# A decoder layer on one core: x loaded first, the first FFN tile computed k by k, the memory projection between the first two tiles

## The reference

```
x <- x + 1/2 * SwiGLU_1(RMSNorm(x))
h  = RMSNorm(x);  projections of h: stick-breaking q,k,v | dilated q,k,v | memory q | 3 gates
A: stick-breaking attention, B: dilated softmax attention
C: cross-attention into the 256 memory tokens: mn = RMSNorm(mem); mk, mv = split(mn @ w_mem_kv); mk = RMSNorm(mk)
x <- x + (sum over the branches of gate * (branch @ w_br)) @ w_out
x <- x + 1/2 * SwiGLU_2(RMSNorm(x))
```

## Time and profile before

| | |
|---|---|
| time, median of 3 runs | 2578.98 us (2578.18 to 2582.18) |
| profiled execution: its time, its span | 2578.72 us, 2576.8 us |
| busy over the span: PE, DVE, ACT, POOL | 97%, 45%, 22%, 8% |
| mean granted TensorE clock | 0.965 of full speed |
| by the page's chain that ended last: PE, DVE, ACT, DMA | 90%, 5%, 2%, 1% |
| data moved by DMA | 125.80 MB, 49 GB/s on average |

### The profile page before, as it was taken

How to read it: one execution, slowest core, us unless ns; L and a number is a source line. 1 busy time by engine, 2 the same in 40 slices (tenths; PEclk the granted TensorE clock), 3 DMA queues, 4 the chain that set the end, 5 groups by cost and what they waited for, 6 DMA issues and landing times.

```text
span 2576.8 us, 25964 instructions
## 1 busy us (share of the span) xinstructions
PE 2492.7 (97%) x10608; PEld 1944.8 (75%) x10608; DVE 1163.4 (45%) x1185; ACT 577.2 (22%) x716; POOL 194.6 (8%) x153
## 2 busy tenths in 40 slices
PE   6999999999999999889999799999999999999998
PEld 5888888888876555446656688887788888888887
DVE  7344444444455665556611432334534444444444
ACT  5211111111123444433322211122311111111111
POOL 2000000000002454320000000001100000000000
PEclk8999999999999999889956899999999999999999
DMA  5211111111112000000100211113111111111112
GB/s 158 72 49 49 49 49 49 49 49 45 45 48 106 17 17 17 8 25 33 33 1 1 66 51 56 49 49 115 41 50 49 49 49 49 49 49 49 49 49 66
DMA packets 48802, 125.80 MB, mean 49 GB/s; under 512 B 4253, under 2 KB 22461, under 8 KB 48480
## 3 DMA queue, kind: packets, MB, share of 16 engines
q1 hardware_dynamic: 45660, 112.88, 14.0%
q10 hardware_dynamic: 2596, 10.89, 1.2%
q0 software_dynamic: 480, 1.10, 0.3%
HBM read 116.42 MB, written 9.87 MB: 49 GB/s over the span
## 4 chain that ended last, share of the span: by engine, by line
PE 90%; DVE 5%; ACT 2%; DMA 1%; issue 1%; POOL 0%; SPq 0%; DVEq 0%; ACTq 0%; POOLq 0%
PE ps L1121 89%; DVE h_lo L743 1%; PE ps L1423 1%; DMA d_st_keep<-d_st 1%; DVE w_lo L736 1%; DVE xT L908 0%; ACT pr_x L534 0%; ACT pr_x L536 0%; DVE pr_x L850 0%; DMA d_fB<-d_f_keep 0%; DVE xT L791 0%; PE ps L1369 0%; DVE d_qk L858 0%; DVE d_qk L853 0%; DVE h_lo L1063 0%
## 5 line engine op out<-in xcount | busy, mean ns | idle before, releaser
L1121 PE MATMUL ps<-h_hi,w_hi 128*128 128x512 f32 x2240 | 888.6, 397 | 25.9 <-DVE o_dil L1056 14.1
L1121 PE MATMUL ps<-h_lo,w_hi 128*128 128x512 f32 x2240 | 876.4, 391 | 0.0
L1121 PE MATMUL ps<-h_hi,w_lo 128*128 128x512 f32 x2240 | 693.6, 391 | 0.0
L1121 PEld LDWEIGHTS ps<-h_hi,w_hi 128*128 128x128 f32 x2240 | 423.5, 189 | 138.3 <-issue 46.0
L1121 PEld LDWEIGHTS ps<-h_hi,w_lo 128*128 128x128 f32 x2240 | 422.8, 189 | 89.2
L1121 PEld LDWEIGHTS ps<-h_lo,w_hi 128*128 128x128 f32 x2240 | 423.5, 189 | 87.1 <-issue 2.2
L474 ACT ACTIVATE w_hi<-raw 128x1024 fp32r<-128x1024 f32 x196 | 204.1, 1051 | 796.6 <-PE ps L1121 786.7
L736 DVE TENSOR_TENSOR w_lo<-raw,w_hi 128x1024 fp32r<-128x1024 f32 x196 | 252.7, 1297 | 167.2 <-ACT w_hi L474 156.8
L791 DVE TENSOR_TENSOR xT<-xT,ps 128x1024 f32<-128x1024 f32 x176 | 214.5, 1218 | 181.2 <-PE ps L1121 181.2
L1121 PE MATMUL ps<-a_hi,w_hi 128*128 128x512 f32 x704 | 275.7, 392 | 5.6 <-DVE w_lo L736 4.9
L1121 PE MATMUL ps<-a_lo,w_hi 128*128 128x512 f32 x704 | 274.7, 390 | 0.0
(11 more groups left out here) (184 smaller groups left out, 1863.3 us busy)
## 6 DMA issues: line engine op xcount, KB each, us to landing
raw<-in_weights SPq DMA_DIRECT2D x196, 512.0 KB, 3.5
x_nat<-in_x SPq DMA_DIRECT2D x8, 512.0 KB, 7.4
x_keep<-xT ACTq DMA_DIRECT2D x1, 4096.0 KB, 12.4
x_back<-x_keep ACTq DMA_DIRECT2D x1, 4096.0 KB, 12.8
out<-y_nat SPq DMA_DIRECT2D x8, 512.0 KB, 3.2
toe_keep<-toe_row ACTq DMA_DIRECT2D x2, 704.0 KB, 6.5
m_nat<-in_mem SPq DMA_DIRECT2D x1, 1024.0 KB, 5.0
d_fB<-d_f_keep POOLq DMA_DIRECT2D x2, 512.0 KB, 7.5
```

What stands on the lines that cost most here:

```text
L1121: return pe.matmul(o, a, b, start=start, stop=stop, skip_group_check=True)
```

## The change

The change rewrites the start of the program, up to the first round of the FFN loop; what comes after is the same instructions in the same order.

- SP loads only rel, oh, the identity and the gains, and then x, with the first two weight units behind x pieces 0 and 1. The memory, the rest of the constants and the head gains come behind x.
- The units are in another order: gate and up of tile 0 are units 0 and 1, the memory's units are 2, 3, 5 and 7, and gate and up of tile 1 are units 4 and 6.
- PE turns x piece 0, makes toe, turns piece 1, and then goes through k = 0 to 7: it turns piece k + 1 and does the 6 matmuls of tile 0's gate and the 6 of its up product for this k, into pairs 0 and 1. At k = 7 it turns the memory tokens in place of a piece of x. The norm's sum follows behind tile 0.
- The memory products 0 and 1 stand ahead of tile 1's gate product, product 2 between gate and up, product 3 behind up; each `proj_aux` follows at some distance.
- ACT and DVE follow the same order. Temporary buffers move in memory.

Core of the diff:

```diff
@@
-U_MEM = 0
-U_FFN1 = U_MEM + 4
+U_MEM = (2, 3, 5, 7)
+U_FIRST = ((0, 1), (4, 6))
+U_LOOP1 = 8
@@ sync
             sp.dma_start(oh[:], onehot).then_inc(onehot_in, 16)
-            sp.dma_start(m_nat[:], mem.rearrange("(b p) d -> p b d", p=P)).then_inc(mem_in, 16)
-            sp.dma_start(cst[:], consts).then_inc(cst_in, 16)
-            sp.dma_start(hg_raw[:], head_gains).then_inc(hgain_in, 16)
+            sp.dma_start(ident, consts[:, 0, :]).then_inc(ident_in, 16)
             sp.dma_start(g_raw[:], gains).then_inc(gain_in, 16)
-            for r in range(NRAW):
-                sp.dma_start(raw[:, r, :], weights[r]).then_inc(raw_in[r], 16)
             for k in range(DT):
                 sp.dma_start(x_nat[:, k], x[:, k * P:(k + 1) * P].rearrange("(b p) c -> p b c", p=P)).then_inc(x_in[k], 16)
+                if k < NRAW:
+                    sp.dma_start(raw[:, k, :], weights[k]).then_inc(raw_in[k], 16)
+            sp.dma_start(m_nat[:], mem.rearrange("(b p) d -> p b d", p=P)).then_inc(mem_in, 16)
+            sp.dma_start(cst[:, 1:7, :], consts[:, 1:7, :]).then_inc(cst_in, 16)
+            sp.dma_start(hg_raw[:], head_gains).then_inc(hgain_in, 16)
@@ scalar
             split_hi(0)
-            split_hi(1)
+            act.wait_ge(gains_ready, 1)
+            for k in range(DT):
+                act.wait_ge(xT_done, k + 1)
+                gain_hi(k, 0)
+                square(0, k)
+                if k == 0:
+                    split_hi(1)
...
+            split_hi(3)
             rstd(0)
...
-            ffn(0, U_FFN1)
+            proj_square(0)
+            split_hi(4)
+            proj_rstd(0)
+            proj_square(1)
+            split_hi(5)
+            proj_rstd(1)
+            silu_tile(0)
+            split_hi(6)
+            split_hi(7)
+            split_hi(8)
+            silu_tile(1)
+            split_hi(9)
+            ffn(0, U_LOOP1 - 2 * GT)
@@ vector
+            def take_x(k):
+
+                dve.wait_ge(x_turned, k + 1)
+                nc.vector.tensor_copy(xT[:, k, :], ps[:, 1 if k == 0 else 2 + k % 2, :]).then_inc(xT_done, 1)
+
+            take_x(0)
+            dve.wait_ge(toe_done, 1)
...
+            split_lo(0)
+            for k in range(DT):
+                if k + 1 < DT:
+                    take_x(k + 1)
+                gain_lo(0, k, 0)
+                if k == 0:
+                    split_lo(1)
...
+            split_lo(3)
...
+            proj_copy(0)
             newton_rstd(0)
 
             dve.wait_ge(toe_out, 16)
-            ffn(0, U_FFN1, lambda m: gain_lo(1, m - 1, 1) if m else None)
+            proj_copy(1)
+            gate_scale(U_FIRST[0][0], 0)
+            split_lo(4)
+            proj_final(0)
+            up_scale(U_FIRST[0][1], 0)
+            split_lo(5)
+            proj_final(1)
+            glu_product(0, 0)
+            split_lo(6)
+            gate_scale(U_FIRST[1][0], 1)
+            split_lo(7)
+            proj_copy(2)
+            proj_final(2)
+            split_lo(8)
+            up_scale(U_FIRST[1][1], 1)
+            split_lo(9)
+            proj_copy(3)
+            proj_final(3)
+            glu_product(1, 1)
+            ffn(0, U_LOOP1 - 2 * GT, lambda m: gain_lo(1, m - 1, 1) if m else None)
@@ tensor
+            pe.wait_ge(ident_in, 16)
+            turn_x(0)
...
             for k in range(DT):
...
+                if k + 1 < DT:
+                    turn_x(k + 1)
+                else:
+                    pe.wait_ge(m_scaled, MB)
+                    pe.wait_ge(xT_done, DT)
+                    for c in range(DT):
+                        for b in range(MB):
+                            last = pe.transpose(ps[:, 2 + c // 4, (c % 4) * MEM + b * P:(c % 4) * MEM + (b + 1) * P],
+                                                m_nat[:, b, c * P:(c + 1) * P], ident)
...
+                pe.wait_ge(h_ready, k + 1)
+                for part in range(2):
...
+                    last = product(part, part, hh, hl, S, k0=k, k1=k + 1)
...
+            pe.wait_ge(cst_in, 16)
+            norm_sum(0)
+            memory(0)
+            memory(1)
+            pe.wait_ge(newton, 1)
+            proj_aux(0)
+            gate_or_up(0, U_FIRST[1][0], 1)
+            proj_aux(1)
+            memory(2)
+            proj_aux(2)
+            gate_or_up(1, U_FIRST[1][1], 1)
+            memory(3)
+            proj_aux(3)
+            pe.wait_ge(pr_final, PR_SB)
+            ffn(0, U_LOOP1 - 2 * GT, 0)
```

More of the change, by code:

```diff
@@ L200, in layer @@
         rB = at("rB", AR + 68 * K, [P, S])
-        pr_mem = [at(f"pr_mem{i}", AR + (46 + i) * K, [P, MEM]) for i in range(3)]
+        pr_mem = [at(f"pr_mem{i}", AR + (4 + i) * K, [P, MEM]) for i in range(3)]
         pr_x = [at(f"pr_x{i}", AR + (56 + 4 * i) * K, [P, S]) for i in range(3)]
@@ L267, in layer @@
         x_in = [sem(f"x_in{i}") for i in range(8)]
[L268 removed]
+        mem_in, ident_in, cst_in, gain_in, hgain_in = (sem(n) for n in ("mem_in", "ident_in", "cst_in", "gain_in", "hgain_in"))
         onehot_in, rel_in = sem("onehot_in"), sem("rel_in")
@@ L772, in glu_tile, with glu_product @@
                                                op0=ALU.mult, op1=ALU.mult).then_inc(up_scaled, 1)
+            def glu_tile(k, t, slot, i=None, between=None):
+                split_lo(k - 1 + AHEAD, i)
+                gate_scale(k - 1, t, i)
+                split_lo(k + AHEAD, i)
+                up_scale(k, t, i)
+                glu_product(t, slot, i, between)
+            def glu_product(t, slot, i=None, between=None):
+                count = at_turn(t, i, 2 * GT)
                 dve.wait_ge(silu_done, count + 1)
@@ L807, in ffn @@
                 t0, g0, u1 = FT * f, NGRP * f, u0 + 2 * GT
-                for q in range(GT):
-                    glu_tile(u0 + 2 * q + 1, t0 + q, q)
+                if f:
+                    for q in range(GT):
+                        glu_tile(u0 + 2 * q + 1, t0 + q, q)
                 with dve.Fori(0, (NGRP - 1) // 2) as i:
@@ L1141, in hl, with gate_or_up @@
                 return h_lo[:, k, :]
+            def gate_or_up(part, k, t, i=None, there=None):
+                pe.wait_ge(split_done, at_turn(k, i) + 1)
+                after(pe, (gate_scaled, up_scaled)[part], at_turn(t, i, 2 * GT))
+                product(part, k % NW, hh, hl, S, there=there).then_inc(unit_done, 1)
             def gate_up(k, t, i=None, there=None, between=None):
-                for part in range(2):
-                    pe.wait_ge(split_done, at_turn(k, i) + part + 1)
-                    after(pe, (gate_scaled, up_scaled)[part], at_turn(t, i, 2 * GT))
-                    product(part, (k + part) % NW, hh, hl, S, there=there if part == 0 else None).then_inc(unit_done, 1)
-                    if part == 0 and between:
-                        between()
+                gate_or_up(0, k, t, i, there)
+                if between:
+                    between()
+                gate_or_up(1, k + 1, t, i)
             def down(g, k, slot, i=None, finish=None):
@@ L1179, in ffn @@
                 t0, g0, u1 = FT * f, NGRP * f, u0 + 2 * GT
-                gate_up(u0, t0, there=lambda k: pe.wait_ge(h_ready, 8 * r + k + 1), between=lambda: norm_sum(r))
-                for q in range(1, GT):
-                    gate_up(u0 + 2 * q, t0 + q)
+                if f:
+                    gate_up(u0, t0, there=lambda k: pe.wait_ge(h_ready, 8 * r + k + 1), between=lambda: norm_sum(r))
+                    for q in range(1, GT):
+                        gate_up(u0 + 2 * q, t0 + q)
                 with pe.Fori(0, (NGRP - 1) // 2) as i:
@@ L1249, in projections, with turn_x @@
                 proj_aux(n1 - 1)
+            def turn_x(k):
+                pe.wait_ge(x_in[k], 16)
+                if k == 1:
+                    pe.wait_ge(toe_kept, 1)
+                elif k == 2:
+                    pe.wait_ge(toe_kept, 2)
+                elif k:
+                    pe.wait_ge(xT_done, k - 1)
+                for b in range(8):
+                    last = pe.transpose(ps[:, 1 if k == 0 else 2 + k % 2, b * P:(b + 1) * P], x_nat[:, k, b, :], ident)
+                last.then_inc(x_turned, 1)
+            pe.wait_ge(ident_in, 16)
+            turn_x(0)
             pe.wait_ge(onehot_in, 16)
@@ L1269, in _, with memory @@
+                pe.wait_ge(h_ready, k + 1)
+                for part in range(2):
+                    if k == 0:
+                        pe.wait_ge(split_done, part + 1)
+                        if part:
+                            pe.wait_ge(xT_done, 1)
+                    last = product(part, part, hh, hl, S, k0=k, k1=k + 1)
+                    if k == DT - 1:
+                        last.then_inc(unit_done, 1)
+            def memory(n):
                 proj(n, lambda k: mT_hi[:, k, :], lambda k: mT_lo[:, k, :],
@@ L1548, in weight_units @@
 def weight_units(w_mem_kv, f1_gu, f1_down, w_in, w_br, w_out, f2_gu, f2_down):
-    units = column_units(w_mem_kv, range(4)) + swiglu_units(f1_gu, f1_down)
```

(3 more changed lines are left out.)

138 lines of the change are left out of this document (54 added, 84 removed).

## The result

The changed kernel took 2598.25 us (median of 4 runs, 2596.91 to 2599.61) against 2579.03 for the kernel before on the same chip (4 runs): ratio 1.0072, 95% interval 1.0055 to 1.009, so 0.7% slower. The prediction was 2600.4 us, range 2590 to 2609. The profiled execution took 2597.82 us.

What follows compares the result with a forecast made beforehand. The prediction took PE's start of the FFN loop as the bound: 66.0 + 6.4 + 48.6 + 4.5 = 125.5 us, 21.7 later than before. Added to the profiled 2578.72 us this gave 2600.4 us, range 2590 to 2609.

Steps and rivals of the forecast that it cites:

- What bounds: Whole program: the effect is when PE begins the FFN loop, 103.81 us before; the rest is the same instructions.
- Part A: Start to tile 0's first product: x lands at 6.8 us, PE starts at 18.9, k = 0 done at 24.3.
- Part B, the ring: Tile 0, k = 1 to 7: turn, copy, h_lo and matmuls follow in turn, 6.2 us per k, to 66.0 us.
- Part B, the clock: Tile 0: four falls to the lower clock after PE's waits, 1.6 us each, 6.4 us; tile done at 72.4.
- first rival: Tile 0 and after: PE's waits close, loop starts at 103.5 or 88.2 us; chance of faster 0.06, within 0.2% 0.04.
- the rival of a fall at every wait: Start: three more clock falls and a larger price before the gate product, 2606.5 us, 2609.7 with late x; chance 0.15.
- The rival without falls: Start: the clock stays up after every wait, 2589.5 us; chance 0.1.
- Part C: Tile 0 to the loop: 48.6 us with waits of 2.9 and 7.9, plus clock falls of 1.6 and 2.9.
- The sum: Start to the loop: 66.0 + 6.4 + 48.6 + 4.5 = 125.5 us against 103.8; time 2600.4 us.
- The rival "PE's waits close": Tile 0: six 2.6 us waits and four falls go; with part C's silu way hidden too, 2563.1 us; faster 0.06.

Runs made afterwards that it cites:

- Experiment 4: Changed kernel with the loads in the order of the kernel before, x last: 2603.82 us, ratio 1.0095 to the kernel before.
- experiment 1: Changed kernel with DVE writing h_lo of piece k ahead of the copy of piece k + 1 in the first tile: 2584.45 us, ratio 1.0022.
- experiments 2: Changed kernel with ACT and DVE re-ordered behind tile 1's gate product, unit 6's split and memory product 2's copies ahead of tile 0's silu: 2588.22 us.
- experiment 6: Changed kernel with the Toeplitz matmuls and their copies ahead of the turn and copy of x piece 0: 2596.37 us, ratio 1.0076.
- experiment 5: Changed kernel with ten extra matmuls that feed nothing, ahead of each product of k = 1 to 6: 2591.05 us, ratio 1.0055.
- version 7: Changed kernel with the reorderings of experiment 1, experiments 2 and experiment 6 together: 2572.02 us, and 2572.55 us when run again.
- experiment 11: On version 7: mT scalings before unit 2's w_lo, ACT's split_hi(4) before the norm's root, unit 4's w_lo after memory copy 0, gate scaling before copy 1: 2569.25 us.

## Why the prediction was right

- **What bounds.** Right: the loop starts 18.4 us later and the span is 19.1 us longer. "The same instructions" behind the loop is right; "the same time" holds for the sum and not for the parts: the merge's first product was 21.8 us later than before (1470.9 against 1449.1), and 2.7 of that came back behind it.
- **Part A.** Right: x piece 0 landed at 7.20 (6.8), the first FFN matmul came at 19.28 (18.9), k = 0 was done at 23.83 (24.3). Experiment 4 gives the early x its own price, 5.7 us.
- **Part B, the ring.** Right in mechanism, shown by experiment 1. A k took 6.41 us (6.2), PE waited 2.51 (2.4 to 2.7). The hand-overs were sized a little small: 1.3 us over six k. Six k had a wait. The prediction has none at k = 7 either, and six in its first rival, yet it bounded the falls by seven: one too many, also in the rival of a fall at every wait.
- **Part B, the clock.** This term was mis-sized. I took four falls of 1.6 us, 6.4 in all. There were two after the waits of 2.51 us, at k = 3 and k = 6, of 1.35 each: 2.7 us. Therefore tile 0 was done at 69.35 and not at 72.4. The rows of before had shown four falls in five waits, but those stretches differ from this ring, and taking their frequency over was the weak step. The rival of a fall at every wait is out: two in six. The profiled executions of experiments 2, 4 and 6, which keep the ring, have two as well, again three products apart. The Trainium skill, page "TensorE: Matmul & The Clock Gate", section "HAM oscillation — how this bites in real kernels", tells of a fall at every single tile in a kernel that waited about 3 to 5 us ahead of each; this ring waits 2.51 us and does not repeat it. The rival without falls is out too, and experiment 5 shows what it would have given: 2.2 us in this stretch.
- **Part C.** 52.9 us from tile 0 to the loop (53.1), by stations 11.4 (11.0), 23.9 (23.7) and 17.5 (18.4). The wait ahead of the gate product was 2.44 (2.9), the one ahead of the transposes 7.95 (7.9). Experiment 2 shows that the order on ACT and DVE made the second. In the last station up product and memory product 3 took 15.05 us, against 13.9 at the upper clock, so the clock cost 1.15 and not 2.9. The two transposes ahead of them (0.69 us) and what stands between them and the loop (1.8 us) took 0.9 more than put down, which takes back half of that.
- **The sum.** 2600.4 against 2598.25, and for the loop 125.5 against 122.22. Of these 3.3 us, 3.7 are clock falls in part B that did not come, against 1.3 of hand-overs; part A gave 0.5, part C 0.2. The later stages took 0.7 us more than in the kernel before. So the total is a little closer than the sum that led to it, which is luck.
- **The rival "PE's waits close".** Did not happen in the change, and its sizes were too large: it put the ring's end at 22.0 us with the loop at 103.5, no change, and both at 37.3 us and 88.2. Measured, against 122.22, were 109.6 for the ring alone (12.6 us) and 100.2 for both (22.0 us). A wait for `mT` of 2.69 us that the ring had covered came out, with the lower clock behind it, and the wait for `w_lo` of unit 4 (2.44 us), which the rival took as gone, stayed. With these two worked on and toe first the loop starts at 92.7.

## What to carry to other kernels

When work is streamed by pieces over several engines, look in each engine's order for a copy of the next piece that stands ahead of the finish of this one: the two make a ring whose period is the sum of all engines' steps, and earlier data does not shorten it. Two lines swapped on DVE turned 6.4 us per piece into 3.9, and with a second such order mended the slower change became 0.24% faster than the kernel before. Before an instruction is moved ahead to close one wait, look at what it waits for itself: `split_hi(4)`, put ahead of the norm's root, held that up for a load. Judge an edit at the start of a long kernel by when the next stage starts, and not by one total: here two later stages of unchanged instructions moved by 3 us each.

## What the runs showed that was not expected

- Stages of unchanged instructions have two durations. Over the 14 profiled executions the stick-breaking stage took 318.5 to 318.9 us nine times and 321.3 to 321.7 five times, and all behind the merge 832.2 to 832.4 five times and 834.7 to 835.0 nine times. The Trainium skill, page "TensorE: Matmul & The Clock Gate", Part 1, says that one kernel shows different numbers of matmuls at the lower clock from run to run; the runs agree (the first 12 FFN matmuls of version 7 took 4.6 and 5.5 us in two executions), and the two stages together can move the total by 0.2%, the size of many tuning steps.
- An earlier start cost time twice. In experiment 6 a first product 3.5 us earlier gave back 2.0 of it, most of that at the lower clock; in experiment 11 the gate product began 0.7 us earlier and ended 1.5 us later, 13.79 against 11.61 us for the same 50 matmuls.
- A DVE subtraction of 1024 columns from two SBUF operands took 2.70 to 2.73 us beside a POOL addition, and 1.22 without.
